# Expert stage: two buffers for raised weight halves instead of three, four for gathered rows instead of three

## The chip, the cores and the metric

The kernel runs on one NeuronCore of one Trainium2 chip. The metric is the device time of one execution in microseconds (us); a kernel's time is the median of its runs. The five engines of the core run their own instruction streams and wait for each other by semaphores: TensorE (PE in the rows; its weight loads are PEld), VectorE (DVE), ScalarE (ACT), GpSimd (POOL) and SyncE (SP), which issues most transfers here.

## What is computed

One layer of a decoder trunk for 256 prompt tokens (with 16 meta tokens ahead of them) and 32 sample tokens, width 2,048: one input projection, RWKV-7 heads and sparse attention heads, an output projection, a layer norm, an expert stage, a second layer norm. The change lies in the expert stage:

```
q = x @ wq                                   # 8 heads, two halves of 128
s = einsum('nhpd,hpkd->nhpk', q, subkeys)    # 128 keys in each half
top 16 of each half, top 16 of their 256 sums -> expert (16,384 experts)
gate = softmax(best_s)
h = gelu(einsum('nd,nhkd->nhk', x, u_tab[expert]))
y = einsum('nhk,nhkd->nd', gate * h, v_tab[expert])
out = layer_norm(ALPHA * x + y)
```

## The kernel before

The expert stage, `peer_layer` (L1931), starts at about 1,532 us. For the 256 prompt tokens it doesn't gather experts: it multiplies by the whole tables and lets a dense array of gates be zero where an expert was not chosen. The tables pass in 256 tiles of 1 MB each: 128 **up** tiles of the table u (128 experts, 2,048 wide), numbered 0 to 127, then 128 **down** tiles of the table v, numbered 128 to 255. For the 32 sample tokens, with 128 partitions for four chosen experts of each, the chosen rows are gathered: 32 gathers of 128 rows (1 MB) from u, then 32 from v.

Every product is made from split numbers. ScalarE writes the raised half of a weight tile (`px_wh`, L2253, `prepare` of the scalar block), VectorE the low half, tile minus raised half, in the place of the loaded tile (`px_w_r`, L2327, `prepare` of the vector block). TensorE adds three products, high by high, high by low and low by high (`split_product`, L272 to L274). Loaded tiles have `SL` = 4 buffers, raised halves have `WH`, gathered tiles `UG`, rows of expert outputs and gates `HS` = 4.

What sets the order is written out by hand, as a loop over u from 0 to 255 on each engine:

- SyncE loads tile u+4 as soon as tile u is multiplied, and in the down part the expert outputs (`px_hid`) and gates (`px_g`) behind it. In the up part it stores the gelu of each tile (`px_h`) to memory.
- ScalarE at turn u raises tile u+2; in the down part also the gate product (`px_gh`, L2257). In the up part it then takes the gelu of tile u (L2274). The raise waits for the load and for the buffer:

```
if u >= WH:
    act.wait_ge(multiplied, u - WH + 1)
act.activation(w_high[u % WH][:], w[s][:], ACT.Copy).then_inc(raised, 1)
```

- VectorE at turn u makes the low half of tile u+2 (in the down part first outputs times gates, L2325), then a step of the key selection (turns 4 to 35), then, in a sample turn, one step for the sample tokens, and in the down part last the low half of the gate product (`lower_gates`, `px_gl`, L2333). Sample turns are every second turn from 42 on in the up part, every third in the down part: 32 products with gathered rows of u (L2439), two short steps, 32 weighted adds of gathered rows of v (L2452), then the second layer norm of the sample rows in nine turns (L2457 to L2473).

```
if u + 2 <= LAST:
    prepare(u + 2)
...
if sample_turn(u):
    next(side, None)
if NK <= u + 2 <= LAST:
    lower_gates(u + 2 - NK)
```

- TensorE multiplies tile u when its low half is there, and in the down part the gate half too (`up`, L2191; `down`, L2204: two token groups of 12 matmuls). In front of every second up tile up to 30 stand a query projection (L2178) and the key scores. The last two down tiles are done for one token group, then for the other.
- GpSimd adds the gates into memory, one expert a token at a time (`expert_gates`, L2122, 256 scatters): 128 ahead of the gathers, then four behind each of the first 32 gathers (`px_fetch`, L2142). A gather waits until the step that reads its buffer's former tile is done.

Of the kernel before, what the change touches and what calls it, by code (L numbers as in the profile page):

```python
# [1924 lines left out]
def peer(cx, a, o, xT, whole, ident, gates_d):  # L1925

    cx.phase(peer_layer, a, o, xT, whole, ident, gates_d)

def peer_layer(cx, a, o, xT, whole, ident, gates_d):  # L1931

    nc = cx.nc
    SL, WH, HS, UG = 4, 3, 4, 3
    NCH = 2 * PH
    CHOSEN_AT = 36
    BEHIND = 4
# [732 lines left out]
```

## Time and profile before

| what | value |
|---|---|
| median of 3 runs | 3165.94 us (3161.84 to 3166.44) |
| the profiled execution's own time | 3163.14 us |
| its span, first to last instruction | 3161.5 us |
| mean granted clock of TensorE over the span | 0.932 |
| busy in the span: TensorE / VectorE / ScalarE / GpSimd | 89% / 57% / 31% / 24% |
| chain that ended last | TensorE 31%, GpSimd 12%, issue 5%, transfers 3% |
| expert stage | 1,532 us to the end; up part to about 2,447 us |

The shares are means over stages with different limits; for this change only the expert stage counts, and in it the question is which wait ends last ahead of TensorE. A start in a row is in us from the span's start. What stands in brackets behind a row is how long the engine was idle before it and what released it. Matmuls overlap: one of 512 columns is shown as 0.39 us while they follow each other every 0.23 us.

### The profile page before, as it was taken

How to read it: one execution, taken by the hardware profiler on the slowest of the kernel's cores; microseconds unless marked ns; L12 is line 12 of the kernel's file. 1: busy time of each engine (PE TensorE's matmuls, PEld its weight loads, DVE VectorE, ACT ScalarE, POOL GpSimd, SP SyncE). 2: the span in 40 equal slices, each digit the busy share in tenths (PEclk: the TensorE clock that was granted, in tenths of full speed). 3: DMA queues.
4: the chain of work that ended last, by engine and by line, in shares of the span. 5: the costliest groups of instructions: out<-in, count | busy, mean ns of one | idle time of the engine just before them, and what ended most of it. 6: DMA issues, size and time to landing. Idle time of an engine off the chain costs nothing.

```text
span 3161.5 us, 45193 instructions
## 1 busy us (share of the span) xinstructions
PE 2820.4 (89%) x17548; PEld 2427.2 (77%) x17548; DVE 1805.1 (57%) x2598; ACT 986.4 (31%) x1169; POOL 772.3 (24%) x630
## 2 busy tenths in 40 slices
PE   3999984767988999759699997999999999999997
PEld 2999972456666666549599997999999888888886
DVE  3455541198774443233468895555656667666655
ACT  1454530011221111122323233333334434434343
POOL 0100002210000222200018787888840000000000
PEclk7999997687889999879899998999999999999999
DMA  3355434322223555242356666999888888876664
GB/s 124 134 185 182 160 142 126 95 68 63 62 67 107 162 154 155 77 145 105 124 166 173 177 180 173 295 300 289 296 309 304 327 303 306 308 275 249 246 237 176
DMA packets 245312, 594.93 MB, mean 188 GB/s; under 512 B 76345, under 2 KB 180162, under 8 KB 192658
## 3 DMA queue, kind: packets, MB, share of 16 engines
q1 hardware_dynamic: 173874, 484.95, 44.8%
q0 software_dynamic: 54592, 90.41, 10.7%
q10 hardware_dynamic: 16640, 16.78, 1.6%
q8 instruction: 135, 2.21, 0.3%
q14 instruction: 71, 0.58, 0.1%
HBM read 535.05 MB, written 56.97 MB: 187 GB/s over the span
## 4 chain that ended last, share of the span: by engine, by line
PE 31%; POOL 12%; issue 5%; DMA 3%; DVE 1%; ACT 0%; DVEq 0%; POOLq 0%
POOL expert_gates L2122 12%; PE px_bank L272 10%; PE px_bank L274 10%; PE px_bank L273 10%; PE px_bank L2178 1%; DMA expert_gates<-px_chosen,px_spot 1%; POOL px_fetch L2142 1%; DMA px_w<-in_peer_v 1%; DMA px_parts<-sample_parts 0%; DMA px_fetch<-in_peer_rows,px_spots_s 0%; ACT px_wh L2253 0%; DMA px_w<-in_peer_wq 0%; DVE px_rows L2514 0%; DMA px_w<-in_peer_u 0%; DVE px_fetch L2519 0%
## 5 line engine op out<-in xcount | busy, mean ns | idle before, releaser
L2327 DVE TENSOR_TENSOR px_w_r<-px_w,px_wh 128x2048 fp32r<-128x2048 f32 x256 | 585.8, 2291 | 278.9 <-ACT px_wh L2253 278.5
L2253 ACT ACTIVATE px_wh<-px_w 128x2048 fp32r<-128x2048 f32 x256 | 489.8, 1913 | 593.1 <-PE px_bank L274 242.3
L272 PE MATMUL px_bank<-px_high,px_wh 128*128 128x256 f32 x2048 | 584.5, 285 | 24.2 <-DVE px_w_r L2327 24.2
L2122 POOL DMA_INDIRECT expert_gates<-px_chosen,px_spot x256 | 499.0, 1949 | 430.3 <-DVE px_chosen L2401 322.9
L273 PE MATMUL px_bank<-px_low,px_wh 128*128 128x256 f32 x2048 | 581.4, 284 | 0.0
L274 PE MATMUL px_bank<-px_high,px_w_r 128*128 128x256 f32 x2048 | 581.4, 284 | 0.0
L272 PEld LDWEIGHTS px_bank<-px_high,px_wh 128*128 128x128 f32 x2048 | 395.2, 193 | 25.6 <-DVE px_w_r L2327 25.6
L272 PE MATMUL px_bank<-px_wh,px_gh 128*128 128x512 f32 x1024 | 398.5, 389 | 1.2 <-DVE px_gl L2333 1.2
L274 PE MATMUL px_bank<-px_wh,px_gl 128*128 128x512 f32 x1024 | 398.4, 389 | 0.0
L273 PE MATMUL px_bank<-px_w_r,px_gh 128*128 128x512 f32 x1024 | 398.4, 389 | 0.0
L273 PEld LDWEIGHTS px_bank<-px_low,px_wh 128*128 128x128 f32 x2048 | 395.2, 193 | 0.0
L274 PEld LDWEIGHTS px_bank<-px_high,px_w_r 128*128 128x128 f32 x2048 | 395.0, 193 | 0.0
L272 PE MATMUL pj_acc<-mixT_r,pj_wh 128*128 128x304 f32 x784 | 244.4, 312 | 44.0 <-DVE pj_w_r L630 44.0
L274 PE MATMUL pj_acc<-mixT_r,pj_w_r 128*128 128x304 f32 x784 | 241.3, 308 | 0.0
L273 PE MATMUL pj_acc<-x_inT_r,pj_wh 128*128 128x304 f32 x784 | 239.4, 305 | 0.0
L272 PEld LDWEIGHTS px_bank<-px_wh,px_gh 128*128 128x128 f32 x1024 | 192.2, 188 | 41.8 <-DVE px_w_r L2327 1.1
L273 PEld LDWEIGHTS px_bank<-px_w_r,px_gh 128*128 128x128 f32 x1024 | 192.2, 188 | 40.0
L274 PEld LDWEIGHTS px_bank<-px_wh,px_gl 128*128 128x128 f32 x1024 | 192.2, 188 | 39.9
L630 DVE TENSOR_TENSOR pj_w_r<-pj_w,pj_wh 128x2048 fp32r<-128x2048 f32 x49 | 112.7, 2302 | 184.0 <-ACT pj_wh L531 184.0
L272 PEld LDWEIGHTS pj_acc<-mixT_r,pj_wh 128*128 128x128 f32 x784 | 149.9, 191 | 48.6 <-DVE pj_w_r L630 44.7
L2439 DVE SCALAR_TENSOR_TENSOR px_fetch<-px_fetch,px_xs 128x2048 f32<-128x2048 f32 x32 | 73.4, 2292 | 142.2 <-DMA px_fetch<-in_peer_rows,px_spots_s 142.2
L2274 ACT ACTIVATE px_h<-px_bank 128x256 f32<-128x256 f32 x128 | 48.8, 382 | 329.2 <-PE px_bank L274 325.5
(392 smaller groups left out, 4352.1 us busy)
## 6 DMA issues: line engine op xcount, KB each, us to landing
px_w<-in_peer_u SPq DMA_DIRECT2D x128, 1024.0 KB, 5.4
px_w<-in_peer_v SPq DMA_DIRECT2D x128, 1024.0 KB, 4.9
pj_w<-in_w_in SPq DMA_DIRECT2D x49, 1024.0 KB, 4.9
expert_gates<-rh_empty ACTq DMA_DIRECT2D x16, 1024.0 KB, 6.4
at_values<-in_kv_pages POOLq DMA_DIRECT2D x128, 128.0 KB, 2.7
at_pages<-in_kv_pages SPq DMA_DIRECT2D x128, 128.0 KB, 2.2
out_w<-in_w_o SPq DMA_DIRECT2D x16, 1024.0 KB, 4.8
px_w<-in_peer_wq SPq DMA_DIRECT2D x16, 1024.0 KB, 4.9
```

What stands on the lines that cost most here:

```text
L272: pe.matmul(out, w_high, high, start=start, stop=False, skip_group_check=True)
L273: pe.matmul(out, w_high, low, start=False, stop=False, skip_group_check=True)
L274: return pe.matmul(out, w_low, high, start=False, stop=stop, skip_group_check=True)
L630: v.tensor_tensor(w_low[c % SL][:], w[c % SL][:], w_high[c % 2][:], ALU.subtract).then_inc(lowered, 1)
L2122: pool.indirect_dma_start(gates_d, bass.IndirectOffsetOnAxis(ap=spot[:, t, z:z + 1], axis=0), chosen[:, 2, t, z:z + 1], None, compute_op=A ...
L2142: pool.indirect_dma_start(fetch[n % UG][:], None, a["peer_rows"] if n < TS else a["peer_v"], bass.IndirectOffsetOnAxis(ap=spots_s[:, r:r + ...
L2178: mm = pe.matmul(acc[:, 0:NY], w[s][:, k * P:k * P + P], xT[:, k, :], start=k == 0, stop=k == KT - 1)
L2253: act.activation(w_high[u % WH][:], w[s][:], ACT.Copy).then_inc(raised, 1)
L2274: act.activation(h[i % HS][:], bank[i % 4][:, 0:NP], ACT.Gelu).then_inc(curved, 1)
L2327: v.tensor_tensor(w_low[s][:], w[s][:], w_high[u % WH][:], ALU.subtract).then_inc(lowered, 1)
L2439: v.scalar_tensor_tensor(to[:], to[:], 1.0, xs[:], ALU.mult, ALU.mult, accum_out=dots[:, r:r + 1]).then_inc(dotted, 1)
```

## The change

`WH` goes from 3 to 2 and `UG` from 3 to 4. Both kinds of buffer are 8 KB a partition, so the memory stays the same. `WH` also counts the raised and low halves of the gate products (`g_high`, `g_low`); `UG` also sets which step a gather waits for.

```diff
-    SL, WH, HS, UG = 4, 3, 4, 3
+    SL, WH, HS, UG = 4, 2, 4, 4
```

No engine's instructions change their order. What changes is which buffer an instruction uses, and so what it waits for. ScalarE in the down part (`px_wh` the raised weight half, `px_gh` the raised gate product, the number behind it the buffer), before:

```order
L2257 ACTIVATE px_gh0_15941<-px_hid1_15934 128x256
L2253 ACTIVATE px_wh0<-px_w2 128x2048
L2257 ACTIVATE px_gh1_15942<-px_hid2_15935 128x256
L2253 ACTIVATE px_wh1<-px_w3 128x2048
L2257 ACTIVATE px_gh2_15943<-px_hid3_15936 128x256
L2253 ACTIVATE px_wh2<-px_w0 128x2048
```

and with the change:

```order
L2257 ACTIVATE px_gh1_15942<-px_hid1_15934 128x256
L2253 ACTIVATE px_wh0<-px_w2 128x2048
L2257 ACTIVATE px_gh0_15941<-px_hid2_15935 128x256
L2253 ACTIVATE px_wh1<-px_w3 128x2048
L2257 ACTIVATE px_gh1_15942<-px_hid3_15936 128x256
L2253 ACTIVATE px_wh0<-px_w0 128x2048
```

A raised half is written over every second tile instead of every third: the raise of tile u waits for the end of tile u-2 instead of u-3. VectorE in the down part, one sample turn and the turn behind it, with the change (`px_w..._r` the low half, `px_fetch` the gathered tile, `px_gl` the low half of the gate product):

```order
L2325 TENSOR_TENSOR px_hid3_15936<-px_hid3_15936,px_g3_15940 128x256
L2327 TENSOR_TENSOR px_w3_r_15932<-px_w3,px_wh1 128x2048
L2452 SCALAR_TENSOR_TENSOR px_acc_s<-px_fetch2,px_bent,px_acc_s 128x2048
L2333 TENSOR_TENSOR px_gl1_15944<-px_hid3_15936,px_gh1_15942 128x256
L2325 TENSOR_TENSOR px_hid0_15933<-px_hid0_15933,px_g0_15937 128x256
L2327 TENSOR_TENSOR px_w0_r_15929<-px_w0,px_wh0 128x2048
L2333 TENSOR_TENSOR px_gl0_15943<-px_hid0_15933,px_gh0_15941 128x256
```

The order is that of before; the add of the sample turn stands between the low half of a tile and the low half of its gate product, both of which TensorE needs.

## Rows read from the trace of the kernel before

**Rows 1.** Windows, down part: length in us, busy PE, PEld, DVE, ACT, POOL, clock, DMA, GB/s
```profile
2600.00:2700.00 100.00, 100.00 (x443) 82.81 (x442) 68.41 (x63) 41.98 (x37) 7.25 (x6) 1.00 0.85 305
```
**Rows 2.** Waits of TensorE in the expert stage: us in total, times, longest
```profile
PE px_bank L272 <- DVE px_w_r L2327: 24.2, 7, 12.6
...
PE px_bank L272 <- DVE px_gl L2333: 1.2, 2, 0.7
```
**Rows 3.** Timeline of SyncE, down part: start, duration, engine, line, operation
```profile
2600.72 0.33 SPq L2090 DMA_DIRECT2D px_w<-in_peer_v  x1
...
2611.60 0.33 SPq L2090 DMA_DIRECT2D px_w<-in_peer_v  x1
...
2617.04 0.33 SPq L2090 DMA_DIRECT2D px_w<-in_peer_v  x1
```
**Rows 4.** Timeline of SyncE, up part
```profile
1636.54 0.33 SPq L2088 DMA_DIRECT2D px_w<-in_peer_u  x1
...
2384.01 0.33 SPq L2088 DMA_DIRECT2D px_w<-in_peer_u  x1
...
2389.77 0.33 SPq L2088 DMA_DIRECT2D px_w<-in_peer_u  x1
```
**Rows 5.** Timeline of TensorE between tiles 158 and 159
```profile
2616.62 0.39 PE L274 MATMUL px_bank<-px_wh,px_gl 128*128 128x512 f32 x1
2616.85 0.39 PE L272 MATMUL px_bank<-px_wh,px_gh 128*128 128x512 f32 x1
```
**Rows 6.** Timeline of ScalarE, raises of tiles 159 and 161
```profile
2608.78 1.92 ACT L2253 ACTIVATE px_wh<-px_w 128x2048 fp32r<-128x2048 f32 x1 [5.77 <-DMA px_w<-in_peer_v]
...
2617.11 1.92 ACT L2253 ACTIVATE px_wh<-px_w 128x2048 fp32r<-128x2048 f32 x1 [0.70 <-PE px_bank L274]
```
**Rows 7.** Timeline of VectorE, tiles 159 and 161
```profile
2615.20 0.42 DVE L2333 TENSOR_TENSOR px_gl<-px_hid,px_gh 128x256 fp32r<-128x256 f32 x1
...
2619.06 2.29 DVE L2327 TENSOR_TENSOR px_w_r<-px_w,px_wh 128x2048 fp32r<-128x2048 f32 x1 [0.23 <-ACT px_wh L2253]
2621.27 0.42 DVE L2333 TENSOR_TENSOR px_gl<-px_hid,px_gh 128x256 fp32r<-128x256 f32 x1
```
**Rows 8.** Groups from 2440 us on, VectorE's adds: busy us, mean ns, idle before
```profile
L2452 DVE SCALAR_TENSOR_TENSOR px_acc_s<-px_fetch,px_bent,px_acc_s 128x2048 f32<-128x2048 f32 x24 | 56.3, 2346 | 0.0
```
**Rows 9.** The same line by source: duration ns least/median/most, first to last start
```profile
L2452 DVE SCALAR_TENSOR_TENSOR px_acc_s<-px_fetch,px_bent,px_acc_s x24: 2343/2346/2351, 2440.8 to 2822.5; 128x2048 f32<-128x2048 f32 x24
```
**Rows 10.** Timeline of VectorE, first step of the sample rows' layer norm
```profile
2843.11 2.28 DVE L2457 TENSOR_TENSOR px_parts<-px_parts 32x2048 f32<-32x2048 f32 x1 [2.14 <-DMA px_parts<-sample_parts]
```
**Rows 11.** Timeline of VectorE and TensorE behind the first product with gathered rows
```profile
1962.10 4.49 DVE L2327 TENSOR_TENSOR px_w_r<-px_w,px_wh 128x2048 fp32r<-128x2048 f32 x2
...
1964.44 0.58 PE L272 MATMUL px_bank<-px_high,px_wh 128*128 128x256 f32 x1 [12.59 <-DVE px_w_r L2327]
```
**Rows 12.** Timeline of ScalarE and GpSimd, raise of tile 10 and first scatter
```profile
1635.29 1.92 ACT L2253 ACTIVATE px_wh<-px_w 128x2048 fp32r<-128x2048 f32 x1 [6.55 <-DMA px_w<-in_peer_u]
...
1645.75 3.46 POOL L2122 DMA_INDIRECT expert_gates<-px_chosen,px_spot  x1 [322.87 <-DVE px_chosen L2401]
```
**Rows 13.** Waits of GpSimd and of VectorE in the expert stage
```profile
POOL px_fetch L2142 <- DVE px_acc_s L2452: 419.5, 29, 24.1
...
DVE px_fetch L2439 <- DMA px_fetch<-in_peer_rows,px_spots_s: 142.2, 32, 20.8
```
**Rows 14.** Timeline of TensorE behind two waits in the up part
```profile
1909.80 0.39 PE L272 MATMUL px_bank<-px_high,px_wh 128*128 128x256 f32 x1 [2.11 <-DVE px_w_r L2327]
1910.02 0.34 PE L273 MATMUL px_bank<-px_low,px_wh 128*128 128x256 f32 x1
...
2164.85 0.39 PE L272 MATMUL px_bank<-px_high,px_wh 128*128 128x256 f32 x1 [1.29 <-DVE px_w_r L2327]
```
**Rows 15.** Windows of 3 us behind these waits, columns as in rows 1
```profile
1909.80:1912.80 3.00, 3.00 (x15) 3.00 (x16) 2.90 (x9) 0.10 (x1) 2.69 (x2) 0.55 0.89 343
2164.90:2167.90 3.00, 3.00 (x25) 3.00 (x26) 2.09 (x1) 1.71 (x1) 2.69 (x2) 1.00 0.96 385
```

## The prediction, made blind

> **What bounds the kernel now.** The change touches the expert stage alone, so first its stretch, 1,532 us to the end, by stretches: in a piece of its down part TensorE is busy all 100 us at granted clock 1.00, with VectorE at 68 and ScalarE at 42 [rows 1]. Next, what ends TensorE's idle time there: 24.2 us in 7 waits for VectorE's low halves and 1.2 us in 2 waits for its gate halves, in 1,630 us [rows 2]. TensorE is the bound; the other engines matter where they make it wait. Below, tile u ends at E(u), the moment its signal reaches the other engines.
>
> Then the pace. In the down part SyncE issues the load of tile u+4 at E(u), so its issues are a clock: E(155) at 2600.72, E(157) at 2611.60, E(158) at 2617.04, that is 5.44 us a tile [rows 3]. In the up part it is 5.76 us [rows 4]. TensorE does not stop between tiles: the last matmul of 158 starts at 2616.62, the first of 159 at 2616.85 [rows 5]. So tile u begins 2616.85 - 2611.60 = **5.25 us after E(u-2)** in the down part. By the same 0.19 us lead it is 5.76 - 0.19 = 5.57 us in the up part.
>
> Last, the chain that readies a tile. ScalarE raises (1.92 us), VectorE takes the low half (2.29) and then the gate halves (0.42) [rows 6, 7]. Every third down tile VectorE does a sample turn between the two: the weighted add, 2.35 us, 24 times in front of a gate half, with no idle time before it [rows 8].
>
> **The change part by part.** No instruction is added, removed or moved; two waits change.
>
> *Two raised halves instead of three.* The raise of tile u needed tile u-3 done and now needs u-2, one tile later. The chain measured from the start of the raise: without a sample turn from 2617.11 to the end of the gate half at 2621.27 + 0.42, 4.58 us; with one from 2608.78 to 2615.20 + 0.42, 6.84 us [rows 6, 7]. The raise starts 0.07 us after SyncE's issue on the same signal (2617.11 against 2617.04) [rows 3, 6], and TensorE starts 0.05 us after VectorE ends (1962.10 + 2.29 to 1964.44) [rows 11]. So a tile is ready 4.70 us after E(u-2) without a sample turn, inside the 5.25, and **6.96 us with one, 1.71 us too late**. The weight load that normally hides behind the last matmul is then exposed; after a stall the next matmul came 0.22 us later (1909.80 to 1910.02) while the pitch is 0.12 (25 in 3 us), so 0.1 more [rows 14, 15]: 1.8 us a sample turn. Before, the same chain from E(u-3) had 5.44 us more, and even with the load late (raise at 2608.78) ended 1.2 us ahead of 2616.85. The stall does not feed on itself: the following tile needs only 4.70 us from a signal that came on time.
>
> Counting. 24 adds stand ahead of a gate half [rows 8]. The first belongs to tile 128, while TensorE is on the last up tile: 0.3 us less slip, 1.5. The other 23: 41.4. After them come five whole-row operations on the 32 sample rows in turns of the same kind (L2457, L2459, L2461, L2467, L2473; the first takes 2.28 us [rows 10]): 5 x 1.8 = 9.0. The short turns among the finish (means, variance, inverse) fit in the 0.55 us of slack. The first of the five already waits 2.14 us for the sample rows to come back from memory [rows 10]; the last add started at 2822.5 [rows 9], so they return 20.6 us after an add begins. Three tiles later with one stall is 3 x 5.44 + 1.8 = 18.1, so it still waits 2.4 us, now on TensorE's path. Sum 54.3.
>
> The end: tile 255 is raised at E(253) instead of E(252), and TensorE wants it half a tile after the start of 254, 12 matmuls of 0.227 us (2616.62 to 2616.85) = 2.7 us instead of 5.44. It is ready at 4.70 against 5.25 - 2.72 = 2.53: 2.3 us with the exposed load.
>
> The up part: chain 0.07 + 1.92 + 0.03 + 2.29 + 0.05 = 4.36 against 5.57, so 1.2 us of slack, and there the sample turn comes behind the low half and is over before the next raise ends. Nothing. Where the queries stand between the tiles there is more room still. From the last query to the first gathered row VectorE is behind with the key selection and may come out up to one tile period, 5.76, later; but TensorE stands 12.59 us at 1964.44 because VectorE waits 20.8 us, its longest, for the first gather [rows 11, 13], and this gather comes when GpSimd is through its scatters. So the cover is GpSimd's chain, and I look at its head: it starts when the first gates are written [rows 12]; that goes back to the raise of tile 10, at 1635.29 when its load landed, now held to E(8), 1636.54 + 0.07 [rows 4, 12]. The whole chain, and TensorE's wait at its end, move by **1.3 us**.
>
> The 1.2 us of gate waits that exist now [rows 2] are in the new stalls: minus 1.2. **Sum: 54.3 + 2.3 + 1.3 - 1.2 = 56.7 us slower.**
>
> *Four gathered tiles instead of three.* GpSimd waited for a free tile 29 times, 419.5 us, always for VectorE's adds, never for the products (L2439), and VectorE never waited for the gather before an add [rows 8, 13]. While the products run, VectorE waits for gathers (142.2 us [rows 13]) because GpSimd sends four scatters between two gathers, not because a tile is lacking. One gather moves forward by a turn at the change of tables. I cost it at nothing; its cover is that the add's gather is issued some 49 us, three turns, ahead. Bounds: no loss beyond one late load, about 3 us (8.06 us from issue at 2600.72 to raise at 2608.78 in a gather's company against 5.44, one period), no gain beyond the 24.2 us of waits.
>
> The bounds of the stall: 1.5 if the small lags vanish, 2.2 if the chain meets a late landing now and then. For 28.5 of them that is 43 to 63, and with the rest +46 to +66.
>
> The profiled execution took 3,163.14 us; 3,163.1 + 56.7 = 3,219.8. It lies 2.8 below the median of the runs, 3,165.94; I add 2 and say **3,222**. This case's own range is 3,208 to 3,238.
>
> (2) *Not slower: the load hides the new wait.* If the loads of the sample-turn tiles landed later than E(u-2), 10.88 us after issue, the raise would wait for them as before and two halves would do: no change, 3,163 to **3,167**. It decides at 10.88; the row shows 8.06 [rows 3, 6], and so late a load would have stalled TensorE already, which it did for 1.2 us. Chance 0.05. The Trainium skill, Trainium Kernel Development and Optimization, section "Best Practices", advises double buffering; by that two halves would suffice and this rival would hold.
>
> (3) *The fourth tile pays.* If a lacking tile held the gathers back, up to the 24.2 us of waits for low halves would go: 3,222 - 24 = **3,198**. Against it stands that GpSimd shows no wait for the products. Chance 0.06. With (2) together it would be faster, about 3,142: 0.03.
>
> **How the numbers follow.** Forecast 0.74, rivals 0.12, 0.05, 0.06, 0.03. Slower by over 0.2% (6 us, about what a measurement of this kernel can tell from no change): 0.74 + 0.12 + 0.06 = 0.92; same 0.05; faster 0.03. The range runs from (3) to a little above (1): 3,198 to 3,250.
>
> **What would show it.** Right: in the down part TensorE waits for the gate halves (L2333) about 29 times, near 1.6 us each; VectorE's low halves follow ScalarE's raise at once; ScalarE's waits for v loads are gone, all are for TensorE; up tiles stay at 5.76 us. Wrong: gate waits much fewer, or between all tiles; a granted clock under 1.00 between 2,450 and 3,140 us; the first product moving by more than 2 us.

## The result, and the profile after

The changed kernel takes **3213.94 us**, median of 4 runs (3197.98 to 3224.98), against 3163.89 us (3159.83 to 3166.44, 4 runs) of the kernel before: 50.05 us slower, ratio 1.0156 with a 95% interval of 1.0105 to 1.0206, which is 33 to 65 us. Forecast were 3,222 us and 56.7 us more. The profiled execution took 3206.46 us, its span is 3204.8.

The expert stage of the changed kernel, TensorE's and ScalarE's waits in it (releaser behind the arrow; us in total, times, longest), then VectorE's and GpSimd's:

```profile
ACT px_wh L2253 <- PE px_bank L274: 1006.6, 249, 12.0
DVE px_w_r L2327 <- ACT px_wh L2253: 586.5, 226, 11.9
POOL px_fetch L2142 <- DVE px_acc_s L2452: 437.7, 28, 24.3
PE px_bank L272 <- DVE px_gl L2333: 50.1, 30, 3.2
DVE px_fetch L2439 <- DMA px_fetch<-in_peer_rows,px_spots_s: 34.2, 14, 4.3
PE px_bank L272 <- DVE px_w_r L2327: 19.3, 11, 3.8
...
PE px_bank L272 <- issue: 1.3, 1, 1.3
```

The fourth line answers to the last of [rows 2]: TensorE's waits for gate halves grew from 1.2 us in 2 to 50.1 us in 30. The sixth answers to the first of [rows 2]: 24.2 us in 7 became 19.3 us in 11, and the 12.6 us wait is gone. GpSimd's wait for a free gathered tile is what it was, with one tile more [rows 13]. ScalarE now waits for TensorE at 249 of its raises, and for no v load any more; before, v loads ended 34 of its waits:

```profile
ACT px_wh L2253 <- DMA px_w<-in_peer_v: 122.4, 34, 10.0
```

Raises are now paced by the freeing of a raised half.

One stalled tile of the down part, by the chain that the prediction went by. SyncE's issue at E(u-2), ScalarE's raise, VectorE, TensorE's weight loads and matmuls:

```profile
2466.34 0.33 SPq L2090 DMA_DIRECT2D px_w<-in_peer_v  x1
```
```profile
2466.41 1.92 ACT L2253 ACTIVATE px_wh<-px_w 128x2048 fp32r<-128x2048 f32 x1 [3.22 <-PE px_bank L274]
```
```profile
2468.36 2.29 DVE L2327 TENSOR_TENSOR px_w_r<-px_w,px_wh 128x2048 fp32r<-128x2048 f32 x1 [2.48 <-ACT px_wh L2253]
2470.57 2.35 DVE L2452 SCALAR_TENSOR_TENSOR px_acc_s<-px_fetch,px_bent,px_acc_s 128x2048 f32<-128x2048 f32 x1
2472.83 0.42 DVE L2333 TENSOR_TENSOR px_gl<-px_hid,px_gh 128x256 fp32r<-128x256 f32 x1
```
```profile
2471.14 0.19 PEld L274 LDWEIGHTS px_bank<-px_wh,px_gl 128*128 128x128 f32 x1
2473.36 0.19 PEld L272 LDWEIGHTS px_bank<-px_wh,px_gh 128*128 128x128 f32 x1 [2.04 <-issue]
```
```profile
2471.36 0.39 PE L274 MATMUL px_bank<-px_wh,px_gl 128*128 128x512 f32 x1
2473.40 0.47 PE L272 MATMUL px_bank<-px_wh,px_gh 128*128 128x512 f32 x1 [1.64 <-DVE px_gl L2333]
2473.70 0.40 PE L273 MATMUL px_bank<-px_w_r,px_gh 128*128 128x512 f32 x1
```

Follow it downwards. The raise starts 0.07 us after the signal, the low half right behind it, then the add, then the gate half, which ends at 2472.83 + 0.42 = 2473.25, 6.91 us after the signal. The weight load starts 0.11 us later, the matmul at 2473.40: 7.06 us in place of the 6.96 predicted. Where the next matmul would have come at 2471.36 + 0.23 = 2471.59, it comes 1.81 us late, and the one behind it follows after 0.30 in place of 0.23: a slip of 1.9 us. The adds' stalls repeat every 18.22 us, from 2455.18 to 2856.11, in place of three tiles of 5.44 us, 16.32: again 1.90 each.

Busy time, clock and DMA in the down part (columns as in [rows 1]):

```profile
2450.00:3140.00 690.00, 642.02 (x2789) 522.85 (x2788) 408.11 (x381) 261.49 (x238) 24.16 (x21) 1.00 0.71 256
2600.00:2700.00 100.00, 90.76 (x395) 73.75 (x396) 60.08 (x57) 37.07 (x34) 7.27 (x6) 1.00 0.75 275
```

The second line answers to [rows 1]: TensorE falls from 100 us of 100 to 90.8, VectorE, ScalarE and the DMA with it (GpSimd does not), and the granted clock there stays at 1.00, the 2.4 GHz level. In the first line 1.00 is a rounded mean. At the longest gate wait, 3.16 us, the clock was at 0.50, the 1.2 GHz level, for 6.83 us (TensorE's matmul behind the wait, and the window):

```profile
2875.85 0.76 PE L272 MATMUL px_bank<-px_wh,px_gh 128*128 128x512 f32 x1 [3.16 <-DVE px_gl L2333]
```
```profile
2874.78:2881.61 6.83, 5.76 (x14) 4.52 (x15) 4.10 (x6) 0.42 (x1) 0.00 (x0) 0.50 0.56 215
```

The next stall, at 2896.82, comes 20.97 us behind this one, 2.7 more than the adds' period of 18.22 and the 0.05 by which its wait, 1.69 us, is longer than theirs: that is what the clock cost here.

**Where the 50 us come from.** The stages ahead of the experts are untouched, but they end at another time in each execution. The first query matmul, the first work of TensorE in the expert stage, stands at

```profile
L2178 PEld LDWEIGHTS px_bank<-mixT,px_w x512: 188/190/338, 1537.6 to 1850.5; 128*128 128x128 f32 x171
```

in the kernel before and at

```profile
L2178 PEld LDWEIGHTS px_bank<-mixT,px_w x512: 188/190/338, 1522.9 to 1835.7; 128*128 128x128 f32 x171
```

in the changed one (line by source; first and last start behind the durations). From there to the span's end it is 3161.5 - 1537.6 = 1623.9 us before and 3204.8 - 1522.9 = 1681.9 after: **58.0 us more in the stage**, of which 14.7 us do not show in the spans because the untouched stages came out that much shorter. I split the stage at the end of tile 127: the up part went from 909.8 to 907.4 us (-2.4), the down part from 714.1 to 774.5 (+60.4).

The same 58 us by what TensorE did in the stage: its idle time grew from 25.4 us in 9 waits to 70.7 in 42, that is 45.3; 33 more waits, each taken at the 0.26 us by which a stalled start slips beyond its idle (1.90 - 1.64), are 8.6; and it worked 23.0 us at a granted clock of 0.50 in place of 13.8, half of which difference is 4.6. The sum is 58.5. With the same three terms taken off, the stages of all ten profiles in this document lie between 1588.6 and 1589.7 us.

### The profile page after: what moved, and what is told of

It is laid out like the page before. It is cut to its first block, busy times and chain, and to the rows that moved or that the text cites. A ratio compares the mean times of both kernels' runs of the same rounds, so it can differ in the third digit from the quotient of the medians.

```text
span 3204.8 us, 45196 instructions
## 1 busy us (share of the span) xinstructions
PE 2823.5 (88%) x17548; PEld 2421.8 (76%) x17548; DVE 1801.4 (56%) x2598; ACT 980.0 (31%) x1169; POOL 776.4 (24%) x630
## 4 chain that ended last, share of the span: by engine, by line
PE 23%; POOL 16%; issue 8%; DVE 3%; DMA 2%; ACT 2%; DVEq 0%; ACTq 0%; POOLq 0%
POOL expert_gates L2122 14%; PE px_bank L272 7%; PE px_bank L274 7%; PE px_bank L273 7%; POOL px_fetch L2142 2%; ACT px_wh L2253 2%; DVE px_acc_s L2452 1%; PE px_bank L2178 1%; DMA expert_gates<-px_chosen,px_spot 1%; DMA px_parts<-sample_parts 0%; DVE px_gl L2333 0%; DMA px_fetch<-in_peer_rows,px_spots_s 0%; DVE px_w_r L2327 0%; DMA px_w<-in_peer_wq 0%; DVE px_rows L2514 0%
## 5 line engine op out<-in xcount | busy, mean ns | idle before, releaser
L272 PE MATMUL px_bank<-px_high,px_wh 128*128 128x256 f32 x2048 | 585.6, 286 | 19.3 <-DVE px_w_r L2327 19.3
L2122 POOL DMA_INDIRECT expert_gates<-px_chosen,px_spot x256 | 485.3, 1896 | 419.2 <-DVE px_chosen L2401 319.2
L272 PE MATMUL px_bank<-px_wh,px_gh 128*128 128x512 f32 x1024 | 402.2, 393 | 51.4 <-DVE px_gl L2333 50.1
L273 PEld LDWEIGHTS pj_acc<-x_inT_r,pj_wh 128*128 128x128 f32 x784 | 150.4, 192 | 0.5
L274 PEld LDWEIGHTS pj_acc<-mixT_r,pj_w_r 128*128 128x128 f32 x784 | 149.1, 190 | 0.0
```

The source lines that it names most:

```text
L272: pe.matmul(out, w_high, high, start=start, stop=False, skip_group_check=True)
L273: pe.matmul(out, w_high, low, start=False, stop=False, skip_group_check=True)
L274: return pe.matmul(out, w_low, high, start=False, stop=stop, skip_group_check=True)
L2122: pool.indirect_dma_start(gates_d, bass.IndirectOffsetOnAxis(ap=spot[:, t, z:z + 1], axis=0), chosen[:, 2, t, z:z + 1], None, compute_op=A ...
```

## The experiments

Each ran 6 to 12 times, beside 26 to 29 runs of the kernel before (median 3161.96 us with the first four, 3161.56 with the other four). Beside the time, each is read by its stage, from the first query matmul to the span's end (1623.9 us before, 1681.9 after), since that leaves out the spread of the stages ahead. The ratios, with their 95% intervals in brackets, are not quotients of the two medians; where the two differ, the interval decides.

**One half of the change: two raised halves.**

```diff
-    SL, WH, HS, UG = 4, 3, 4, 3
+    SL, WH, HS, UG = 4, 2, 4, 3
```

> Only the raised halves go to two; the gathered tiles stay at three. Theory A (the later raise plus the sample turn ahead of the gate half): all of the slowdown is here, some 50 to 57 us over the kernel before, and about 30 waits of TensorE for gate halves (L2333) of 1.6 us in the down part, as with the whole change. Rival B (the fourth gathered tile costs, by transfers that collide): under 35 us over before, the rest missing.

Measured: 3218.56 us, ratio 1.0183 (1.0153 to 1.0214), stage 1682.3. TensorE's waits:

```profile
PE px_bank L272 <- DVE px_gl L2333: 50.8, 30, 3.9
...
PE px_bank L272 <- DVE px_w_r L2327: 18.6, 11, 3.8
```

They are close to those of the changed kernel, 50.1 us in 30 and 19.3 in 11. The whole slowdown is the two raised halves': rival B falls, and with it the rival by which late loads hide the wait.

**The other half: four gathered tiles.**

```diff
-    SL, WH, HS, UG = 4, 3, 4, 3
+    SL, WH, HS, UG = 4, 3, 4, 4
```

> Only the gathered tiles go to four; raised halves stay at three. Theory A: GpSimd never waited for a free gathered tile while the products ran, so nothing moves: within 4 us of the kernel before. Rival B: 10 us or more slower. Rival E (the gathers were held back by the tiles): 10 to 24 us faster, with the first product and TensorE's 12.6 us wait earlier.

Measured: 3155.1 us, ratio 0.9998 (0.9975 to 1.0021), stage 1628.4. The fourth tile changes nothing that can be measured, which here means nothing beyond 8 us faster or 7 slower. Its profile has one long gate wait:

```profile
PE px_bank L272 <- DVE px_gl L2333: 6.8, 1, 6.8
```
```profile
2824.19 0.42 DVE L2325 TENSOR_TENSOR px_hid<-px_hid,px_g 128x256 f32<-128x256 f32 x1 [12.00 <-DMA px_g<-expert_gates]
```

VectorE had waited 12.00 us for that tile's gates to arrive. In none of the other nine profiles, four of them with four gathered tiles, does TensorE stand so long behind late gates; whether the fourth tile has to do with it one execution doesn't tell.

**Which of the two waits?** WH sizes the raised weight halves and the raised and low gate halves alike. Here only the gate halves drop to two, with a wait of their own (VectorE's and TensorE's uses of them go by `GH` too):

```diff
+    GH = 2
...
+                        if j >= GH:
+                            act.wait_ge(multiplied, NK + j - GH + 1)
-                        act.activation(g_high[j % WH][:], hid[j % HS][:], ACT.Copy).then_inc(g_raised, 1)
+                        act.activation(g_high[j % GH][:], hid[j % HS][:], ACT.Copy).then_inc(g_raised, 1)
```

> Raised weight halves stay at three, the halves of the gate products go to two, gathered tiles three. Theory A: the raise starts as before, the gate product's halves are 0.4 us each and come in time: within 4 us of the kernel before, at most 3 waits of TensorE for gate halves. Rival C (it is the gate product's buffer that delays the gate half): 40 us or more over before, with about 29 waits of 1.6 us for L2333.

Measured: 3160.85 us, ratio 1.0007 (0.9981 to 1.0033), stage 1621.4. In its trace (lines 3 further down) TensorE waits for gate halves once:

```profile
PE px_bank L272 <- DVE px_gl L2336: 0.8, 1, 0.8
```

So it is the raise of the *weights* that comes too late; the gate half is only the last link.

**Take the add out of the chain.** The changed kernel, and in the vector loop the gate half ahead of the sample turn; nothing else:

```diff
-                    if sample_turn(u):
-                        next(side, None)
                     if NK <= u + 2 <= LAST:
                         lower_gates(u + 2 - NK)
+                    if sample_turn(u):
+                        next(side, None)
```

> The changed kernel (two halves, four gathered tiles), with VectorE's gate half put ahead of the sample turn in the loop. Theory A: a down tile is then ready 4.70 us after the signal of the tile two before, inside 5.25, whether it has a sample turn or not, so the waits for L2333 go, but for the last tile's 2.3 us: 0 to 6 us over the kernel before. Rival D (two halves are too few by themselves, whatever stands between): still 25 us or more over before, with waits for the low or gate halves at most down tiles.

Measured: 3160.44 us, ratio 1.0004 (0.9985 to 1.0022), stage 1630.5. TensorE's waits, and VectorE at one sample turn:

```profile
PE px_bank L272 <- DVE px_w_r L2327: 18.5, 11, 3.8
...
PE px_bank L272 <- DVE px_gl L2333: 7.2, 3, 4.5
```
```profile
2463.55 2.29 DVE L2327 TENSOR_TENSOR px_w_r<-px_w,px_wh 128x2048 fp32r<-128x2048 f32 x1 [2.48 <-ACT px_wh L2253]
2465.76 0.42 DVE L2333 TENSOR_TENSOR px_gl<-px_hid,px_gh 128x256 fp32r<-128x256 f32 x1
2466.10 2.35 DVE L2452 SCALAR_TENSOR_TENSOR px_acc_s<-px_fetch,px_bent,px_acc_s 128x2048 f32<-128x2048 f32 x1
```

The add still runs, with two raised halves as in the changed kernel, but TensorE no longer waits for it. All 24 stalls at adds are gone, and those at the finishing steps with them. What stays are the return of the sample rows (4.50 us), 0.59 us a little later, and 2.10 us at the last tile. The stage is still 6.6 us longer than before, with as much idle time of TensorE (25.7 us against 25.4): it worked 24.4 us at a granted clock of 0.50 in place of 13.8, 6.8 of them at the waits of 4.50 and 2.10 us.

**The same order in the kernel before.** The same edit with three raised halves.

> The kernel before (three halves, three gathered tiles) with VectorE's gate half ahead of the sample turn. Control for the swap by itself. Theory A: with three halves a down tile is ready some 3 us early either way, so the swap changes nothing: within 4 us of the kernel before. Rival G (the swap helps for a reason of its own, so that its effect on the changed kernel doesn't show the cause): 10 us or more faster than before.

Measured: 3157.5 us, ratio 0.9996 (0.9976 to 1.0016), stage 1622.5. With three halves the order does not matter: what the swap brought above is what the two halves had cost, and no gain of its own that can be measured.

**The size of the stall.** The changed kernel with the weighted add over 1,024 of its 2,048 columns, which leaves half of the sample tokens' sum out:

```diff
-                        v.scalar_tensor_tensor(acc_s[:], fetch[n % UG][:], bent[:, r:r + 1], acc_s[:],
-                                               ALU.mult, ALU.add).then_inc(added, 1)
+                        v.scalar_tensor_tensor(acc_s[:, 0:1024], fetch[n % UG][:, 0:1024], bent[:, r:r + 1],
+                                               acc_s[:, 0:1024], ALU.mult, ALU.add).then_inc(added, 1)
```

> The changed kernel with each of the 32 weighted adds cut to 1024 of 2048 columns (half of the sample tokens' weighted sum is left out). Theory A (a stall is what the chain exceeds 5.25 us by): the add falls from 2.35 to about 1.2 us, the chain from 6.96 to about 5.8, so the 23 waits for L2333 at adds fall from 1.64 to about 0.5 us, those at the five finishing steps stay at 1.6 to 3.2; 22 to 28 us faster than the changed kernel, 25 to 32 over before. Rival H (a wait costs a fixed handshake whatever stands in front): the waits stay above 1.2 us and the kernel stays 40 us or more over before.

Measured: 3196.71 us, ratio 1.0108 (1.0083 to 1.0134), stage 1657.7, 24.2 us under the changed kernel's. The add, and the matmul that waited for the gate half behind it:

```profile
2469.19 1.28 DVE L2452 SCALAR_TENSOR_TENSOR px_acc_s<-px_fetch,px_bent,px_acc_s 128x1024 f32<-128x1024 f32 x1
```
```profile
2470.95 0.47 PE L272 MATMUL px_bank<-px_wh,px_gh 128*128 128x512 f32 x1 [0.58 <-DVE px_gl L2333]
```

The add is 2.35 - 1.28 = 1.07 us shorter, the stall 1.64 - 0.58 = 1.06, and the stalls now come every 17.15 us, 1.07 less. The stall is the excess of the chain over its time, microsecond for microsecond, and no fixed cost of having two buffers. The 23 adds alone would give 24.6 us and the first add 1.1. The sample rows made TensorE wait 7.47 us where it was 3.16, against the expectation: VectorE's first step on them started 22.93 us behind the start of the last add in place of 19.68. The longer wait gave 4.3 us back, and the up part was 3.4 us shorter. By the medians the run is 35.2 us over before and 17.2 under the changed kernel, outside the 25 to 32 and the 22 to 28 expected; the stage's 24.2 is inside the second and its 33.8 over before outside the first.

**A start four turns later.** The kernel before, with the sample turns of the up part from tile 50 instead of 42, because TensorE's longest wait, 12.59 us [rows 11], stands at a product whose gathered rows GpSimd has not sent yet:

```diff
-            return u >= 42 and u % 2 == 0
+            return u >= 50 and u % 2 == 0
```

> The kernel before with sample turns from up turn 50 instead of 42, all else as it was. Theory A: the first gather lands some 40 us ahead of its product, so TensorE's wait for it (12.6 us in the profile of before, 7 in two later ones) and the small waits between the products go, the key selection's 9 us stay: 6 to 16 us faster than before. Rival I (GpSimd's chain only moves its wait elsewhere, to the transfer of the gates at the start of the down part): within 4 us of before, with a new wait near tile 128.

Measured: **3146.14 us, ratio 0.9946 (0.9921 to 0.9971)**, stage 1605.2. It is faster than both kernels. TensorE's only waits for VectorE in the stage are

```profile
PE px_bank L272 <- DVE px_w_r L2327: 9.0, 4, 3.8
```

all in the key selection, where VectorE is busy 38.7 of the 40 us from 1870 to 1910; no new wait stands near tile 128. The 15 us at the products are gone, and the medians differ by 15.4. That the two agree so well is partly chance: in the three other profiles with three halves and a start at 42 the waits at the products are 10.8 to 11.7 us, and the interval is 9 to 25 us.

**Both repairs on the changed kernel.** Two halves, four gathered tiles, the swap, and the start at tile 50.

> The changed kernel (two halves, four gathered tiles) with both edits: gate half ahead of the sample turn, and sample turns from up turn 50. Theory A: no 1.6 us waits in the down part, 2.1 us at the last tile, up to 4.5 us where the sample rows come back; the waits between the products go: 0 to 10 us faster than before. Rival D: 25 us or more slower than before.

Measured: 3156.94 us, ratio 0.9983 (0.9965 to 1.0001), stage 1622.1.

```profile
PE px_bank L272 <- DVE px_w_r L2327: 11.6, 6, 3.8
...
PE px_bank L272 <- DVE px_gl L2333: 6.1, 3, 3.4
```

With the products' waits gone, the key selection's is 2.6 us longer than with three halves, and 6.1 us of gate waits are left: the third half is worth something even in the good order. The two rows leave 8.7 us more idle than the run before this one; the stage is 16.9 us longer. The other 8 us are the clock: TensorE worked 26.8 us at a granted clock of 0.50 where the run before this one has 10.8, and half of the difference is 8.0. At the wait where the sample rows come back, 3.4 us, the window is

```profile
2898.77:2905.60 6.83, 5.90 (x14) 4.69 (x15) 3.99 (x6) 0.91 (x2) 0.00 (x0) 0.50 0.52 204
```

while with three halves the run before this one stayed at 1.00 from the end of the key selection on:

```profile
1913.00:3128.00 1215.00, 1212.86 (x7373) 1092.21 (x7372) 751.44 (x597) 487.41 (x441) 382.43 (x207) 1.00 0.81 283
```

## Why the prediction was right

The sign, the mechanism and the size held: 56.7 us were forecast for the stage, 58.0 came in the profile, and of the signs named in advance the stalls, their lengths and the raises paced by TensorE came as written, the clock all but for one stretch of 6.83 us. By its steps:

- *A stall of 1.8 us at each weighted add.* Right in place and number: one of 1.28 us at the first add (put by the trace to the engine itself), then 23 of 1.64, forecast about 1.55 idle. The slip is 1.90 in place of 1.8. The undersized part is the hand-over from VectorE to TensorE, which I took from a row behind a low half as 0.05 us [rows 11]; it is 0.15 here, 0.11 to the start of the weight load and 0.04 from there to the matmul. 23 x 0.1 is 2.3 us.
- *Five finishing steps, 9.0, and the sample rows' return, 2.4.* The five waits are 3.16, 1.69, 1.70, 1.76 and 1.63 us. The first has 3.16 - 1.64 = 1.5 us for the return. It was sized too large by 0.9: VectorE started on the rows 19.68 us behind the start of the last add, not 20.6, and had itself waited 1.38 us. A sixth wait of 0.25 us was costed at nothing: ScalarE was at the sample rows' squares (L2278), so a raise started 0.96 us behind its signal.
- *The last tile, 2.3.* It waited 2.10 us, and with the 0.26 by which every slip here exceeds its idle that is 2.4. The two runs with two halves and the swap show the same 2.10: this stall has no add in it. With the slips of 1.90 put for every wait, the down part adds up to 1.5 + 43.7 + 9.5 + 1.5 + 0.25 + 2.4 - 1.2 = 57.7 of its 60.4 us; the rest, 2.7, is the half clock at the 3.16 us wait.
- *The stall does not feed on itself.* Right: the waits stay at 1.64 over 400 us.
- *GpSimd's chain and the first product, +1.3.* **This step failed.** The head of the chain moved as forecast, from 108.1 to 109.3 us after the first query matmul (1645.75 - 1537.6 [rows 12], 1632.2 - 1522.9). But the scatters behind it, and VectorE, did not stay as they were. From the start of the first scatter to the end of the 128th it took 284.0 us in place of 298.5, and the first product came 9 us earlier within the stage; I had named 2 us as the limit. The kernel before's profile is the odd one: the other profiles have 290.6 to 290.9 us with three halves and 284.0 to 287.8 with two, shorter in every one; why, these runs don't show. And VectorE is ready for the first product 413 us after the first query matmul with two halves, 401 to 402 with three: 12 us later, where I had put 5.76 at most. So the 12.59 us cover on which the step rested was one execution's, and the lag used it up. With three halves other profiles have 7.1 to 7.5 us there, and with two 1.9 us at most, while in those the key selection waits 11.5 to 11.7 us in place of 9 and some later products 1.2 to 1.7 us each. In all, where the turns start at tile 42, TensorE waits for low halves 16.2 to 19.3 us in 9 to 11 with two halves and 19.8 to 24.2 us in 7 to 9 with three. So the two halves cost a little in the key selection, against a forecast of nothing there, and pay it out of a wait that would have come anyway. The up part as a whole was 2.4 us shorter, not 1.3 longer; but that is the odd profile again. From the first query matmul to the start of the last up matmul it takes 909.4 us there, 905.8 to 907.6 in the three others with three halves, and 906.4 to 907.0 in three with two: no difference. That the errors cancelled is luck: the down part was 5 us over its sum, the up part 4 under.
- *The fourth gathered tile, nothing.* Shown by the run with it alone, to within its 7 or 8 us.
- *The bounds.* They don't follow from the working: +46 to +66 on 3,163.1 is 3,209 to 3,229, not 3,208 to 3,238. The measured 50.05 lies inside +46 to +66.

**The rivals.** The clock (0.12) fell in size, not in kind: the stalls at the adds ran at 1.00, but the one wait of 3.16 us brought half clock and 2.7 us in the down part, where the rival had 23. The Trainium skill, TensorE: Matmul & The Clock Gate, section "A second HAM failure mode: psum-queue depth-cycling", tells of a kernel in which short idles between matmul groups, coming often enough, swing the clock. Here idles of 1.64 us every 18 us did not. The late load (0.05) fell with the run of two halves alone. The Trainium skill, Trainium Kernel Development and Optimization, section "Best Practices", advises "Double-buffer for performance: Overlap DMA with compute". It speaks of transfers, and these buffers stand between engines, so this case doesn't test it; that two would suffice here, as the prediction draws from it, did not hold in this order of work. The fourth tile (0.06) fell with its run.

The medians differ by 50.05 us, less than the stage's 58.0; the interval of 33 to 65 holds both, and the stages ahead, behind which the first query matmul came between 1518.3 and 1539.8 us in these profiles, are enough to make the difference.

## What to carry to other kernels

How many buffers a stage needs is read by comparing two times: from the signal that frees a buffer to the moment when the tile in it is ready, and from that signal to the moment when the bound engine wants it. Two buffers did for tiles with 4.7 us against 5.25 and failed by the excess at every third tile, whose chain had 2.35 us of other work in it. Before buying a buffer, look at what stands in the chain without belonging there: moved behind the link that the bound engine waits for, the same work stalled nothing with two buffers. The third buffer still kept a few waits away, and the half clock that came with the longer of them. And a wait that covers a cost in one profile is to be looked for in a second one before it is counted on.

## What was not expected of the hardware

Of the thirty idles of TensorE at gate halves 29, most of them of 1.64 us and one every 18.2 us, left its granted clock at 1.00, and the one of 3.16 us had 0.50 with it for 6.83 us. Over the ten profiles every idle of 3.16 us or more in the stage had a stretch at 0.50 with it, and none of those up to 1.76 us in the down part. Between them both happen: the 2.10 us at the last tile were followed by 0.50 in three of five profiles, and in the up part of the kernel before an idle of 2.11 us was followed by 0.55 for 3 us [rows 15] and one of 2.04 us, 26 us earlier, was not. What tells these apart the runs don't show. A mean of 1.00 over 690 us did not show the fall; a window around the longest wait did. A stalled start costs more than its idle: slip 1.90 us, idle 1.64. GpSimd's scatters, all of one shape, took from 1.53 to 3.67 us each, and 128 of them from 284.0 to 298.5 us. Ahead of them the same code, unchanged in all ten profiles, ended at times 21.5 us apart, which is why single spans of this kernel say little and stages are compared here.
